# Last-layer attention scores split into 64-row and 32-row products, reordered expansion columns, moved DMA orders, and halved first and last transfers

## The reference, cut to what matters

```
kv = (rms_norm_2(kv_a, kv_a_norm) @ w_kv_b).reshape(B, n, 16, 64 + 64)      # k_nope, v
q  = rms_norm_2((rms_norm_2(q_a, q_a_norm) @ w_q_b).reshape(B, n, 16, 64 + 32), q_norm)
s  = (einsum('bqhd,bkhd->bhqk', q_nope, k_nope)
      + einsum('bqhr,bkr->bhqk', q_rope, k_rope)) * 96 ** -0.5
o  = einsum('bhqk,bkhd->bqhd', softmax(s), v)        # 512 queries, 256 + 512 keys
```

## Time and profile before

| | us |
|---|---|
| median of three runs | 1862.41 |
| the profiled execution | 1869.95 |
| its span | 1868.2 |
| TensorE matmuls busy | 1775.8 (95%) |
| TensorE weight loads busy | 993.2 (53%) |
| VectorE busy | 756.3 (40%) |
| ScalarE busy | 549.0 (29%) |
| GpSimd busy | 154.0 (8%) |

### The profile page before, as it was taken

How to read it: one execution, slowest core, us unless ns; L and a number is a source line. 1 busy time by engine, 2 the same in 40 slices (tenths; PEclk the granted TensorE clock), 3 DMA queues, 4 the chain that set the end, 5 groups by cost and what they waited for, 6 DMA issues and landing times. The chain is left out here.

```text
span 1868.2 us, 24014 instructions
## 1 busy us (share of the span) xinstructions
PE 1775.8 (95%) x9586; PEld 993.2 (53%) x9586; DVE 756.3 (40%) x1469; ACT 549.0 (29%) x1121; POOL 154.0 (8%) x194
## 2 busy tenths in 40 slices
PE   8999888998989989999999999999999999999998
PEld 3333465464544444555464444577645544577763
DVE  2244378142521121333234224577524327466542
ACT  2111478123100111333224111455312232344420
POOL 2110001001111110111100014000000003000000
PEclk9999989989999999999999999999999999999999
DMA  7654948438999999999970231000201012000001
GB/s 272 225 208 170 137 121 80 161 127 338 420 416 416 417 416 418 419 416 417 402 294 5 85 116 65 1 2 1 99 7 35 23 62 79 12 1 1 2 23 45
DMA packets 92047, 324.81 MB, mean 174 GB/s; under 512 B 12296, under 2 KB 28808, under 8 KB 64928
## 3 DMA queue, kind: packets, MB, share of 16 engines
q1 hardware_dynamic: 78080, 302.55, 44.2%
q10 hardware_dynamic: 8656, 12.32, 1.9%
q0 software_dynamic: 5200, 8.41, 1.2%
HBM read 317.58 MB, written 14.30 MB: 178 GB/s over the span
## 5 line engine op out<-in xcount | busy, mean ns | idle before, releaser
L1061 PE MATMUL mix_ps<-arena 128*64 128x256 f32 x2048 | 236.6, 384 | 7.7 <-DMA arena<-in_w 3.4
L2137 PE MATMUL tail_ps<-arena 128*128 128x512 f32 x504 | 220.6, 594 | 0.0
L1061 PEld LDWEIGHTS mix_ps<-arena 128*64 128x64 f32 x2048 | 144.5, 137 | 93.5 <-issue 22.8
L949 PE MATMUL mix_ps<-arena,side 128*128 128x512 f32 x384 | 174.5, 607 | 1.4 <-DVE side L1415 1.4
L463 DVE TENSOR_REDUCE tail_small<-tail_ps 128x1 f32<-128x768 f32 x128 | 116.6, 952 | 120.6 <-PE tail_ps L337 120.6
L2137 PEld LDWEIGHTS tail_ps<-arena 128*128 128x128 f32 x504 | 95.1, 191 | 114.8 <-issue 114.3
L1073 PE MATMUL mix_ps<-arena 128*64 128x512 f32 x512 | 116.9, 598 | 23.5 <-DMA arena<-in_w 23.5
L949 PEld LDWEIGHTS mix_ps<-arena,side 128*128 128x128 f32 x384 | 71.8, 193 | 102.2 <-issue 84.0
L2137 PE MATMUL tail_ps<-arena,side 128*128 128x512 f32 (+2 forms) x320 | 119.6, 534 | 0.0
L553 ACT ACTIVATE arena<-tail_ps,tail_small 128x768 f32<-128x768 f32 x128 | 113.7, 898 | 4.7 <-DVE tail_small L463 4.7
L337 PE MATMUL tail_ps<-side,arena 96*128 96x512 f32 (+1 forms) x256 | 90.9, 498 | 6.4 <-ACT arena L553 5.8
(11 more groups left out here) (384 smaller groups left out, 2356.6 us busy)
## 6 DMA issues: line engine op xcount, KB each, us to landing
arena<-in_w SPq DMA_DIRECT2D x96, 2048.0 KB, 21.5
arena<-in_l_w_mod SPq DMA_DIRECT2D x16, 1024.0 KB, 5.0
arena<-in_l_w_in SPq DMA_DIRECT2D x16, 1024.0 KB, 7.2
arena<-in_w_in SPq DMA_DIRECT2D x12, 1024.0 KB, 9.1
arena<-in_l_w_mod SPq DMA_DIRECT2D x16, 512.0 KB, 4.6
residual<-bias_blocks SPq DMA_DIRECT2D x32, 224.0 KB, 10.9
arena<-in_l_w_in ACTq DMA_DIRECT2D x12, 512.0 KB, 11.0
arena<-in_l_w_out SPq DMA_DIRECT2D x6, 1024.0 KB, 5.4
```

Source lines behind the costliest of these rows:

```text
L949: last = pe.matmul(ps[:, u % 4], oT[:, k, t * P:(t + 1) * P], weights.slot(W_IN[n, k // 4], 4, 512)[:, k % 4], start=(k == 0), stop=(k == ...
L1061: last = pe.matmul(out[h * CAP:(h + 1) * CAP, 0:H2], x, wb[:, k, h * H2:(h + 1) * H2], start=(k == 0), stop=(k == DK - 1))
L2137: last = pe.matmul(out, lhs(k), rhs(k), start=(k == 0), stop=(k == K - 1))
```

## The change

1. The expansions' columns are reordered on the host: all 16 heads' 64 plain query columns, then all 16 heads' 32 rotated ones; the keys and values of a pair of heads as k, k, v, v. The norms follow (two reductions and two scalings for a query tile in place of one of each, one more addition of 64 sums, the cosine product as two instructions).
2. A group's turns are four pieces: plain queries of both heads in one (4 transpositions of 128 columns), rotated queries (8 products with the identity, each placed twice, at rows 0 and 64), and keys of both heads in whole tiles (6 transpositions). The rotated keys are turned in group 0 alone, placed at rows 0, 32, 64 and 96 (24 products).
3. The scores of a unit are four products with 64 rows and four with 32 rows, each over 384 of the 768 keys. Head x uses rows 64x to 64x + 63, then rows 64z + 32x for half z. Maximum and exponential read two banks with 384 columns in each.
4. In the first layer: tile 0 of x is turned and gained in halves; `consts` is ordered after the second `modulate`; the two halves of the bias table are written in two places; the table is read only after the last `modulate`.
5. The last tile of the output is stored in two halves.

```diff
@@ scores(n)
+            if self.rotated is not None:
+                half = (hi - lo) // 2
+                for z in range(2):
+                    for x in range(L):
+                        q, k = self.score_parts(g, x, t, lo + half * z, lo + half * (z + 1))
+                        pe.matmul(self.scores_of(n, x)[:, z], q, k, start=True, stop=False)
+                for x in range(L):
+                    for z in range(2):
+                        q, k = self.rotated(g, x, t, z)
+                        ins = pe.matmul(self.scores_of(n, x)[:, z], q, k, start=False, stop=True)
+                    ins.then_inc(s["scored"], 1)
+                return
@@ turn(g, js)
+                        for row, cols in src:
+                            ins = pe.matmul(Tp[row:row + cols.shape[-1], bank, z * P:(z + 1) * P], cols, m["ident"], start=True, stop=True)
@@ mla_turn(p)
+        def twice(x):
+            return [(0, x), (64, x)]
+        pieces = [([q[t][:, P * p:P * (p + 1)] for t in range(XT)], P, [qn[:, p % 2]]), ([twice(q[t][:, 1024 + 64 * p:1024 + 64 * (p + 1)]) for t in range(XT)], P, [qr[:, p % 2]])]
+        if p == 0:
+                pieces.append(([[(r, kr[:, t]) for r in range(0, P, 32)] for t in range(a, e)], P, [krT[:, a * P:e * P]]))
+            pieces.append(([kv[t][:, 256 * p:256 * p + P] for t in range(a, e)], P, [kn[:, p % 2, a * P:e * P]]))
@@ block.sync
             sp.wait_ge(s["normed"], 16)
+            sp.wait_ge(s["mod_mm"], 3 * DK)
             for g in range(2):
                 table_in(g)
@@ block.scalar
-            act.wait_ge(s["loaded"][0], 16)
-            act.dma_start(cst[:], A["consts"]).then_inc(s["small_in"], 16)
...
             act.activation(sd_x, ss_x, ACT.Sqrt, bias=m["eps"], scale=1.0 / D).then_inc(s["sd_x"], 1)
+            act.wait_ge(s["mod_mm"], 2)
+            act.dma_start(cst[:], A["consts"]).then_inc(s["small_in"], 16)
...
-                    if (n, t) == (2, 1):
+                    if (n, t) in ((2, 1), (3, 1)):
                         act.wait_ge(s["shifted"], 1)
-                        for b in range(2):
+                        for b in (n - 2,):
@@ block.vector
-            gain_x(0)
+            for b in range(2):
+                dve.wait_ge(s["x_turned"], b + 1)
+                dve.tensor_tensor(oT[:, 4 * b:4 * b + 4, 0:P], ps[:, 6 + b].rearrange("p (k t) -> p k t", k=4), ...)
@@ the output
+            for cc in range(2):
+                sp.wait_ge(*emptied(("z", XT - 1, cc)))
+                sp.dma_start(rows(A["out"])[XT - 1][:, cc * 512:(cc + 1) * 512], hx[:, XT - 1, cc * 512:(cc + 1) * 512]).then_inc(s["stored"], 16)
```

More of the change, by code:

```diff
@@ L248, in __init__ @@
         self.spread = spread
+        self.rotated = rotated
         self.N, self.groups, self.PRB = len(units), len(turns), LEAD + 1
@@ L321, in turn @@
                 for z, src in enumerate(sources):
[L322 removed]
+                    if isinstance(src, list):
+                        for row, cols in src:
+                            ins = pe.matmul(Tp[row:row + cols.shape[-1], bank, z * P:(z + 1) * P], cols, m["ident"], start=True, stop=True)
+                    else:
+                        ins = pe.transpose(Tp[0:rows, bank, z * P:(z + 1) * P], src, m["ident"])
                 ins.then_inc(s["turned"], 1)
@@ L921, in turn_x @@
                 if t:
-                    pe.wait_ge(s["x_gained"], t)
+                    pe.wait_ge(s["x_gained"], t + 1)
                 for k in range(DK):
+                    if t == 0 and k == 4:
+                        last.then_inc(s["x_turned"], 1)
                     last = pe.transpose(ps[:, 6 + k // 4, k % 4 * P:(k % 4 + 1) * P], hx[:, t, k * P:(k + 1) * P], m["ident"])
@@ L944, in _ @@
                     for k in range(DK):
+                        if n == 0 and k == 4 and t == 0:
+                            pe.wait_ge(s["x_gained"], 2)
                         if n == 0 and k == 4 and t + 1 < XT:
@@ L2611, in _ @@
             chain(inverse_root(dve, chain, st_q[:, 0], st_q[:, 1], 96, st_q[:, 3], st_q[:, 2]))
-            xq = lambda t: q[t].rearrange("p (h d) -> p h d", d=96)
+            xq = lambda t: (q[t][:, 0:1024].rearrange("p (h d) -> p h d", d=64), q[t][:, 1024:1536].rearrange("p (h d) -> p h d", d=32))
             def scale(t):
-                dve.tensor_tensor(xq(t), xq(t), st_q[:, 2, 16 * t:16 * (t + 1)].unsqueeze(2).to_broadcast([P, 16, 96]), ALU.mult).then_inc(s["scaled_1"], 1)
+                for x in xq(t):
+                    last = dve.tensor_tensor(x, x, st_q[:, 2, 16 * t:16 * (t + 1)].unsqueeze(2).to_broadcast(list(x.shape)), ALU.mult)
+                last.then_inc(s["scaled_1"], 1)
                 dve.wait_ge(s["scaled_1"], 1 + t + 1)
```

62 lines of the change are left out of this document (36 added, 26 removed).

## The result

| | before | after |
|---|---|---|
| median, us | 1862.90 (6 runs, 1862.11 to 1866.16) | 1854.01 (6 runs, 1852.21 to 1856.91) |
| the profiled execution, us | 1869.95 | 1853.95 |
| its span | 1868.2 | 1852.2 |

The ratio is 0.9947 [0.9935, 0.9960], 9.9 us; the medians lie 8.9 us apart. Forecast were 17.8 (1844.6, range 1837 to 1852). Two later comparisons gave 0.9944 [0.9926, 0.9962] and 0.9947 [0.9927, 0.9966], with medians 11.3 and 9.5 us apart. The profiled execution of before lies 7 us above its median and that of after on its median, so the 16 us between the two spans are not the gain. The table takes three profiles on each side, by the start of each stage's first product on TensorE. The kernel "first layer only" has the old attention and the new head, so its first row belongs to the new side.

What follows compares the result with a forecast made beforehand. TensorE, with matmuls filling 95% of the span, was taken as the bound. Savings of 11.2 + 0.7 + 0.7 + 4.6 + 0.6 = 17.8 us off the median 1862.4 gave 1844.6, range 1837 to 1852.

Steps and rivals of the forecast that it cites:

- The terms for the last attention: Last attention: 11.2 us saved in scores over 32 units, 0.7 in turns, 0.7 as group 1 stops turning rotated keys.
- The head: First layer: four waits of TensorE, for a gain, weights and transfers, shorten or go; 4.6 us saved (2 to 5.2).
- the end: Span's end: half the bytes remain to store after the last order; 0.6 us saved (0 to 1.3).
- the 0.20 on top belong to two changes of tile shape, in and out, 0.10 each: Price read from the grouped attention's 64-row scores; it put the last attention's new scores at 2.24 us for 2.59.
- The turns: Later groups of the last attention: first turn step 0.12 us more, second 0.22 less; 0.7 saved over seven groups.
- Group 0: Last attention's first group: turning costs 1.27 us more ahead of the last gate product, 1.2 less afterwards; net 0.
- Does a plain step get it?: Last attention's steps without turns: ScalarE's copy gates, not the maxima, so the full 0.35 us is saved; period 5.44.
- Rival 2: Last attention: the maxima take over the 18 steps without turns; 3.6 us less gain, 1848.2 in all; chance 0.13.
- Rival 1: Last attention's scores: each change of shape is a full drain, 2.42 us; 5.8 less saved, 1850.4; chance 0.13.
- Rival 4: Last attention: 32-row products don't run side by side; 1.94 us more a step, 1907 in all; chance 0.05.
- the come-back near 35: First layer: part of the time won at the first product and second `modulate` returns as a wait, 0.6 us.
- Rival 3: First layer: waits only move to the next weights, or experts' transfers absorb them; 4 us less, 1848.6; chance 0.12.

## Why the prediction was wrong

The direction was right, and so was what bounds the steps; the size of the largest term was not. The terms for the last attention add up to 12.6 us (11.2 + 0.7 + 0.7). Of these some 6 came: 5.8 by the means of three profiles on each side (216.6 to 210.8), 6.5 by the profiles without a stretch at the lower clock (216.2 to 209.7). The head and the end came as forecast. So 6.1 to 6.8 of the 17.8 are missing in the attention, which leaves 11.0 to 11.7 where 9 to 11 were measured. The rest, some 2 us, is not placed: the stretch up to the last experts alone varies from 714 to 721 us in the table, whatever the kernel.

**The step that failed: "the 0.20 on top belong to two changes of tile shape, in and out, 0.10 each".** The 0.20 of the earlier trace rows is what one stretch of side-by-side products has on top of its columns: the half change on its way in and the half on its way out. The other halves fall to the neighbours and were invisible there, since they are inside the values or the transpositions. A change between two tiled stretches, 64 to 32 rows, costs both halves. So the new scores are 1.30 + 0.20 + 0.65 + 0.20 = 2.35, not 2.24. Two more places in every group follow, which the sum had left out because it took changes as belonging to the scores alone:

- The weights' transpositions now have such a neighbour on both sides: 1.46 for 1.40. In the plain steps this is the 3.26 from transpositions to scores (1638.24 to 1641.50), for 3.20.
- The turns. To the engine the old ones were whole tiles, those of 128 x 64 too: the values ahead of them take 1.46, as ahead of any other shape (1.37 where the same shape follows), and the 96-row scores follow them without a price. So an old turned step had two changes, weights to values and values to turns. The new first step has turns of two shapes and then 64-row scores: four transpositions take 0.58 for 0.45, and the turn is 1.61 for the forecast 1.47. In the second step six transpositions take 0.80 for 0.68. So the turns, forecast at 0.7 saved, cost 1.1: 7 x (0.26 - 0.10).

Counted over a group this way, the kernel before has 8 changes of shape (two a unit, into the values and out of them) and the changed one 19 (four a unit, and three more in the two turns). The columns that went are worth 2.8 us a group (3072 columns of scores and two transpositions) and a group became 0.72 shorter, so the 11 changes cost 0.19 each. The prediction counted three a unit as new; new are two, but each at about twice its price.

**Where the price stands in the trace.** It shows in the weight loads of TensorE, which run beside the products. Timeline of PEld: the first two lines are of before (the transpositions behind 96-row scores start at 1649.26, the scores behind the 128 x 64 turns at 1646.67), the others of after.

```profile
1649.04 1.45 PEld L349 LDWEIGHTS tail_ps<-first,arena 128*128 128x128 f32 x12
1646.57 0.30 PEld L337 LDWEIGHTS tail_ps<-side,arena 96*128 96x128 f32 x2
...
1637.38 0.31 PEld L351 LDWEIGHTS tail_ps<-side,arena 32*128 32x128 f32 x8 [0.54 <-issue]
...
1638.24 1.29 PEld L370 LDWEIGHTS tail_ps<-first,arena 128*128 128x128 f32 x12 [0.55 <-issue]
...
1639.70 1.29 PEld L384 LDWEIGHTS tail_ps<-residual,arena 128*64 128x64 f32 x24 [0.17 <-issue]
```

In the first two places nothing is lost, and the first load of the stretch starts 0.22 and 0.10 us ahead of its first product. In the other three, which are changes of shape, it starts with the product (1637.38 for 1637.39, 1638.24 and 1639.70 for the same), after 0.17 to 0.55 us in which nothing is loaded. So the price goes along with loads that no longer run ahead. Whether that is all of it, or the array must also run empty first, these rows don't show.

**Group 0** gave almost nothing either. Compare the second profile of before with the second of after, in which the clock stayed up. From the first turn to the first scores: 11.40 and 11.68 (forecast: no change). From the first scores to the second: 5.34 and 5.38, since a longer wait, 2.95 for 2.53, takes what the shorter scores give (forecast: 0.35 less). From the second to the third: 6.35 and 5.95 (by the terms of the forecast 0.9 less, with the rotated keys that group 1 no longer turns). Together 1.2 us short; the other 4.9 of 6.1 fall to the rest of the attention. Timeline of TensorE behind that wait, in the first profile of after, with its granted clock (us, busy us of each engine, granted clock of TensorE, DMA share, GB/s):

```profile
1597.15 2.93 PE L347 MATMUL tail_ps<-side,arena 64*128 64x384 f32 x8 [2.95 <-ACT arena L575]
...
1597.15:1601.60 4.45, 4.45 (x16) 1.70 (x16) 0.00 (x0) 0.00 (x0) 0.00 (x0) 0.50 0.00 0
```

and in its second profile:

```profile
1604.84 1.56 PE L347 MATMUL tail_ps<-side,arena 64*128 64x384 f32 x8 [2.95 <-ACT arena L575]
```

In the first, TensorE ran at the lower of its two levels, 1.2 GHz, and the scores took 4.46 for 2.35; in the second the granted clock is 1.00 behind the same wait, and they took 2.35. The kernel before does both too: 4.05 us for its second scores in the first profile, 2.68 in the second, both behind 2.5 us of waiting. The prediction took this slow stretch, which it read in the earlier trace rows, for a fixed cost; it came in seven of the fourteen profiles. That is why the last attention varies by 1 to 2 us.

Point by point, the rest:

- *Does a plain step get it?* Yes: what the scores save less the 0.06 of the transpositions, 0.18 behind a turned step (5.61 for 5.79) and 0.25 elsewhere (5.52 for 5.77). The wait in front of the scores is still for VectorE's copy or ScalarE's exponential (0.27 and 0.18), not for a maximum. Rival 2 falls. The 2.59 of the old scores, read "with nothing lost", holds behind transpositions; behind the values they took 2.66 to 2.68, so the old kernel paid for a change there as well.
- *Rival 1* (a full drain at each change, S = 2.42) was nearest in kind and size (2.35 measured, 2.24 forecast). The Trainium skill (TensorEngine Tiling, "Key Properties") says that a change of tiling mode drains the engine. The runs agree in that each change costs time: 0.20 in the scores, 0.15 in the turns. The prediction had read the same rule as a small price; the rule gives no number, and the kernel with two more changes in each unit does.
- *Rival 4* falls: the four products with 32 rows stand side by side, 0.86 for the eight records.
- *The head* came as written in its first profile, the come-back near 35 too (0.81 at 36.49; 0.6 expected). That it fits to 0.1 us is partly luck, as the waits there vary by 2 us; the mean over the profiles is 4.6 too. Rival 3 falls in its first form: the gain reaches the attention. One reading was off: the first product's 6.48 us are 1.8 times the later 3.60, not twice.
- *The norms, the end*: the first turn follows the gate products without a wait (cost 0, as forecast); the end is 0.6 shorter, as forecast.
- *Not foreseen:* at the last expert TensorE waits longer for `in_w`, then computes slowly. Timeline of after:

```profile
926.72 5.35 PE L1101 MATMUL mix_ps<-arena 128*64 128x512 f32 x16 [2.10 <-DMA arena<-in_w]
...
948.62 3.69 PE L2175 MATMUL tail_ps<-extra,arena 128*128 128x256 f32 x16 [2.53 <-PEq L164]
```

and of the kernel with the first layer's part only:

```profile
924.25 3.65 PE L1079 MATMUL mix_ps<-arena 128*64 128x512 f32 x16 [0.66 <-DMA arena<-in_w]
929.37 14.05 PE L1230 MATMUL mix_ps<-extra,arena 128*128 128x256 f32 x64 [1.46 <-issue]
945.95 5.38 PE L2147 MATMUL tail_ps<-extra,arena 128*128 128x256 f32 x16 [2.53 <-PEq L164]
```

The wait is 1.44 longer. Behind it the same 16 records take 5.35 for 3.65; the granted clock of that stretch (926 to 933) is 0.76 in the mean, where it is 1.00 in the other kernel (924 to 929.2). 1.46 of this is covered by an idle stretch behind it. So the stage is 1.6 longer. It stands in the ten profiles with the full new attention and in none of the other four (three with the old attention, one without the 32-row half), although the expert code is the same in all. So it is hardly chance, but its cause is open; the first layer's part alone doesn't bring it. It is not a loss of the whole, though. The first product behind the experts, after the same wait of 2.53, takes 3.69 for 5.38, at a granted clock of 1.00 for 0.67, so that 1.6 to 1.7 come back at once; this holds in eight of the ten. The one slow stretch has moved ahead by one product.

## What to carry to other kernels

Price a stretch of side-by-side products by its columns plus 0.20 us, and count changes of shape over the whole step with its neighbours, turns and transpositions included, not only in the instruction group that changes. When a row shows an overhead "in and out", ask whether the neighbours hold the other half; a kernel that alternates on purpose (here twice more a unit, 0.845 a stretch) prices it in one run. Compare single stages only between profiles with the same granted clock in them. And where TensorE is the bound, a copy doubled on an idle engine (ScalarE, 29%) is cheaper than a product doubled on TensorE: 4.5 us of the last attention here, 7.5 between the medians, for one line.

## What the runs showed of the hardware beyond that

- Four 32-row products side by side, float32, 384 columns each, have 0.65 us of columns in eight records and take 0.86 with their changes of shape. Adding to banks that 64-row products opened just before has no price of its own: stretches that add and stretches that don't both take 0.845.
- The half change inside transpositions of whole tiles is smaller: twelve of them take 1.35 between whole tiles (1793.41 to 1794.76 in before), 1.40 with one change beside them and 1.46 with two.
- Full-height tiles with 96 rows or 96 columns behave as whole ones: the earlier trace rows have 12 such transpositions in 1.35, and scores behind them with nothing lost. A float32 transposition of 128 x 64 does too (eight in 0.90, scores behind them with their weights loaded ahead); a product of the same 128 x 64 shape does not, it goes with the values.
- A wait of 2.95 us ahead of TensorE can cost twice: in some executions it was followed by 4.46 us for 2.35 of work at the lower clock, in others by nothing.
